# Two-layer block kernel: large-product operands placed at multiples of 512 bytes, vectors split into two tables

## The chip, the cores and the metric

The kernel runs on one core of a Trainium2 chip. The metric is the device time in microseconds (us) of one execution, as a median over runs; the profiled execution is a single one, seen through its trace. PE is TensorE, DVE is VectorE, ACT is ScalarE, POOL is GpSimd, SP is SyncE.

## The reference, cut to what matters

Two transformer-like layers for 256 tokens of width 1024, all in float32. The parts with large matrices are these:

```python
proj = h @ w_in[l]                              # layer 1: 1024 -> 2568
x = x + concat([o, pool_out]) @ w_out[l]        # 1024 -> 1024
q = (xb @ w_query)                              # 1024 -> 2048
...                                             # top 16 of 128 x 128 experts for each of 8 heads
u = expert_down[idx]; v = expert_up[idx]        # 16384 experts of width 1024
act = gelu(einsum("td,thkd->thk", xb, u))
y = einsum("thk,thkd->td", gate * act, v)
...
proj = h @ w_in_2                               # layer 2: 1024 -> 3584
x = x + mix @ w_out_2
u = causal_dwconv(h @ w_up, conv_w, conv_b)
x = x + (gelu(u) * (h @ w_gate)) @ w_down       # 1024 -> 2816 -> 1024
g = sigmoid(rmsnorm(x) @ w_ple_gate);  x = x + (p @ w_ple) * g
```

The kernel computes the expert layer densely: all 16384 experts for all tokens, multiplied by a table of gates that is zero where an expert was not chosen.

## The kernel before, in words

All large matrices lie in memory as 412 tiles of 128 x 1024 float32 (512 KB). SP loads them in one order into four slots, `raw`. For each tile ACT writes the rounded part `whi` (type fp32r, `split_hi`) and DVE the rest `wlo = raw - whi` (`split_lo`), both in rings of four slots. The activations are split in the same way: `ahi`/`alo` for an operand of 1024 features, `phi`/`plo` (two slots of 256 tokens each) for the products of the expert layer's second half and of the feed-forward layer's second half, `pthi`/`ptlo` for the small embedding product. Each product of float32 numbers is then three products of fp32r (`products`): high x high, high x low, low x high.

A tile is used in one of two ways:

- `gemm_tile`: the weights are stationary. For each of 8 slices `k`, the 128 x 128 slice of `whi` or `wlo` is loaded into the array and 256 columns of `ahi`/`alo` are streamed: 24 products of 128x256 for each tile. Layer 1's input (20 tiles), the queries (16), the experts' first half (128), layer 2's q, k and retention parts (20) and the feed-forward layer's first half (44) go this way.
- `token_rows`: the activations are stationary. A 128 x 128 slice of `ahi`/`alo` or `phi`/`plo` is loaded and 512 columns of `whi`/`wlo` are streamed: 12 products of 128x512 for each tile. With `ahi` stationary: the output projections and the values (8 tiles each) and most of the last gate. With `phi` stationary: the experts' second half (128 tiles) and the feed-forward layer's second half (22 tiles).

There is no scheduler: each engine's program is written out in order and waits on counting semaphores. The matrices' order sets the stages; the list below names those that the prediction speaks of.

- Stage of the experts' first half (span's time about 220 to 600 us): PE makes `gemm_tile` after `gemm_tile`; DVE picks the top 16 and splits tiles; from the first pick on POOL issues 256 indirect DMAs (`scatter`, L409) that add the gates of one head, one choice and one block of 128 tokens each into the table `gates_dense` in memory. Before the first one of a head it waits until the previous head's have landed.
- Stage of the experts' second half (about 604 to 961 us), 128 tiles: for each tile `n` ACT copies `ea` row `n` to `phi` (`p_hi`), which waits until PE has finished tile `n - 2`; DVE makes `plo` (`p_lo`), then splits a weight tile, then multiplies row `n + 2` of `ea` with the gates in `gd` (`apply`, L1850). SP loads `gd` four tiles at a time from `gates_dense` (`gates_of`) in between the weight loads. The tokens of the second block are gated from this table only from tile `SPLIT` = 88 on: so before the pair of loads for tile 88 SP waits for all the scatters of that block (`scat1`, the wait after `up_pair`'s first loop), and everything that SP loads later, weights too, stands behind that wait.

Where the tensors lie in a partition is set by `place`: it hands out addresses one after another from the first free byte, 16512, rounding sizes up to 32 bytes. Worked out from the code, the starts before, with their remainders:

| tensor | start before | mod 512 | mod 64 |
|---|---|---|---|
| `raw`, `whi`, `wlo` | 16512, 32896, 49280 | 128 | 0 |
| `ahi`, `alo` | 65664, 73856 | 128 | 0 |
| `phi`, `plo` | 94176, 96224 | 480 | 32 |
| `pthi`, `ptlo` | 215136, 217184 | 96 | 32 |
| `ea`, and with it `h32`, `sq` | 98272, 98272, 106464 | 480 | 32 |
| `TT`, `X` (plain float32) | 193472, 181184 | 448 | 0 |
| `gw_hi` (8 columns a slice) | 218048 | 448 | 0, 32 in turn |

All slices of `whi`, `ahi` and `phi` that the products take begin a multiple of 512 bytes behind the tensor's start, so a slice has the remainder of its tensor.

Of the kernel before, what the change touches and what calls it, by code (L numbers as in the profile page):

```python
# [16 lines left out]
F32R = mybir.dt.float32r  # L17
F16 = mybir.dt.float16
U32 = mybir.dt.uint32
ALU = mybir.AluOpType  # L20
# [4 lines left out]
T = 256  # L25
TB = T // P
D = 1024
KT = D // P
# [47 lines left out]
CV = {}  # L76
_c = 0
for _n, _w in (("norm_mix", KT), ("conv", 48), ("dn_norm", 1), ("pool_scale", PG), ("norm_ffn", KT), ("norm_mid", KT),
# [2 lines left out]
    CV[_n] = _c  # L81
    _c += _w
N_CV = _c

# [13 lines left out]
def program(nc, x_tok, vecs, wts, c1, gate_w, rows, w_pool, keys, c2, ple_t, nrows, out):  # L100
    ctx = ExitStack()
    with ctx:
        s = {n: ctx.enter_context(nc.semaphore("s_" + n)) for n in SEMS}


        top = [-(-nc.sbuf_base // 32) * 32]
        slab = ctx.enter_context(nc.sbuf_tensor("slab", [P, (nc.sbuf_bytes_remaining - 64) // 4], F32))

        def place(name, shape, dt=F32, at=None):
            size = int(np.prod(shape)) * (2 if dt == F16 else 4)  # L110
            size = -(-size // 32) * 32
            if at is None:
                at, top[0] = top[0], top[0] + size
            else:
                at[0], at = at[0] + size, at[0]
            return nc.alloc_sbuf_tensor_at(name, [P] + list(shape), dt, offset=at)

        raw = place("raw", [2, 2 * TW])
        whi = place("whi", [RING, TW], F32R)
        wlo = place("wlo", [RING, TW], F32R)  # L120
# [1 line left out]
        alo = place("alo", [KT, T], F32R)  # L122
        ident = place("ident", [P])
        ones = place("ones", [P])
        vec = place("vec", [N_CV])
        warm = place("warm", [8])
        wm = place("wm", [KT])
        eps = warm[:, 6:7]
        small = top[0]
        xt = place("xt", [TB, D])  # L130
        pf = place("pf", [2, T])
        aux_end = top[0]
        phi = place("phi", [2, T], F32R)
        plo = place("plo", [2, T], F32R)
        aux = [small]
        v16 = place("v16", [TB, 2, TOPK], at=aux)
        i16 = place("i16", [TB, 2, TOPK], U32, at=aux)
# [12 lines left out]
        aux = [small + 4 * KT * T]  # L150
# [3 lines left out]
        aux = [small]  # L154
# [2 lines left out]
        iota = place("iota", [P, GT], F16, at=aux)  # L157
        oh1 = place("oh1", [2, 2, SPLIT, GT], F16, at=aux)
        assert aux[0] <= small + 4 * KT * T
        aux = [aux_end]  # L160
        oh2 = place("oh2", [2, P, GT], F16, at=aux)
        oheq = place("oheq", [2, SPLIT, GT], F16, at=aux)
        assert aux[0] <= top[0]
        aux = [small]
        gd = place("gd", [2, 4, T], at=aux)
        assert aux[0] <= small + 4 * KT * T
        arena = top[0]
        ea = place("ea", [N_EXP, T])
        end = top[0]
        assert end <= nc.sbuf_usable_end, end  # L170

        a = [arena]
        h32 = place("h32", [KT, T], at=a)
# [55 lines left out]
        c = 0  # L229
# [55 lines left out]
            return bank((0, 1, 6, 7, 2, 3, 4, 5)[b0], n, base)  # L285

        def vcol(name, j=0):
            return vec[:, CV[name] + j:CV[name] + j + 1]

        def b3(ap, n):  # L290

# [25 lines left out]
        def _(sp):  # L317
            sp.dma_start(xt[:, 0, :], x_tok[:, 0, :]).then_inc(s["x_in"], 16)
            sp.dma_start(xt[:, 1, :], x_tok[:, 1, :]).then_inc(s["x_in1"], 16)
            sp.dma_start(vec[:, :], vecs).then_inc(s["vec_in"], 16)  # L320
            rs = (s["raw0"], s["raw1"], s["raw2"], s["raw3"])
            for j in range(4):
                if j == 1:
# [108 lines left out]
        def split_hi(act, u, j, quad=None):  # L432

            if quad is None:
                if u >= N_TILES:
                    return
                act.wait_ge((s["raw0"], s["raw1"], s["raw2"], s["raw3"])[j], 16 * (u // 4 + 1))
                if u >= RING:
                    act.wait_ge(s["w_used"], u - RING + 1)
            else:  # L440
                act.wait_ge((s["raw0"], s["raw1"], s["raw2"], s["raw3"])[j], quad * 16 + 16)
                act.wait_ge(s["w_used"], quad * 4 + (j - RING + 1))
            nc.scalar.activation(whi[:, j, :], raw_tile(j // 2, j % 2), ACT.Copy).then_inc(s["w_hi"], 1)  # L443

        def split_lo(dve, u, j, quad=None):

            if quad is None:
                if u >= N_TILES:
                    return
                dve.wait_ge(s["w_hi"], u + 1)  # L450
                if u >= RING:
                    dve.wait_ge(s["w_used"], u - RING + 1)
            else:
                dve.wait_ge(s["w_hi"], quad * 4 + (j + 1))
                dve.wait_ge(s["w_used"], quad * 4 + (j - RING + 1))
            nc.vector.tensor_tensor(wlo[:, j, :], raw_tile(j // 2, j % 2), whi[:, j, :].bitcast(F32),  # L456
                                    ALU.subtract).then_inc(s["w_lo"], 1)
# [75 lines left out]
        def turned_dve(dve, n, q, weight):  # L533
# [5 lines left out]
            m.then_inc(s["operand"], 1)  # L539

        mix_weight = lambda k: vcol("norm_mix", k)
        peer_weight = lambda k: vcol("norm_ffn", k)
        mid_weight = lambda k: wm[:, k:k + 1]
        ffn_weight = lambda k: vcol("ffn_norm", k)
        ple_weight = lambda k: vcol("ple_norm", k)

# [559 lines left out]
        def _(act):  # L1106
# [21 lines left out]
            act.wait_ge(s["t_pre"], 1)  # L1128
            row_root(0, 1, 2, pre[:, 0, 0:1])
            split_hi(act, 0, 0)  # L1130
            act.wait_ge(s["vec_in"], 16)
            for q in range(4):
                turned_act(act, 0, q, mix_weight)
            for u in range(1, LEAD):
# [357 lines left out]
        def _(dve):  # L1492
            V = nc.vector
            ch = Chain(dve, s["dve_step"])
# [24 lines left out]
                V.tensor_scalar(half_row(h32_t, b0), half_row(xt, b0), r_col[:, 0, 1:2], None, ALU.mult)\  # L1519
                 .then_inc(s["yd"], 1)  # L1520
            split_lo(dve, 0, 0)
            dve.wait_ge(s["vec_in"], 16)
            for q in range(4):
                turned_dve(dve, 0, q, mix_weight)
            for u in range(1, LEAD):
# [2 lines left out]
            def lo_for(u):  # L1528
                split_lo(dve, u + LEAD, (u + LEAD) % 4)

            ch(V.tensor_tensor(wm[:, :], vec[:, CV["norm_mid"]:CV["norm_mid"] + KT],
                               vec[:, CV["attn_norm"]:CV["attn_norm"] + KT], ALU.mult))
            bv = lambda n: col[n].rearrange("p (n h) -> p n h", n=TB)
            bav = col["ba"].rearrange("p (n c) -> p n c", n=TB)

# [653 lines left out]
```

## Time and profile before

| what | value |
|---|---|
| median of three runs | 1329.02 us (1328.91 to 1329.16) |
| span of the profiled execution, first to last instruction | 1327.4 us |
| PE busy with matmuls | 1310.4 us, 99% of the span |
| PE loading stationary operands | 1196.9 us, 90% |
| DVE / ACT / POOL busy | 943.1 / 725.3 / 517.7 us |
| memory traffic | 253.03 MB, mean 191 GB/s |
| granted TensorE clock, mean | 0.998 |

No other time of the profiled execution is recorded than its span; the median of the runs is 1.6 us above it. The busy time of PE is a sum of overlapping instructions: a matmul's shown duration is its latency, and the next one starts before it ends. How fast PE works is therefore read from the distance between the starts of matmuls, or from their count in a stretch.

### The profile page before, as it was taken

Reading aid. Unit: us, or ns where it says so; the run is one execution under the profiler, and the core shown is the slowest. Engines: PE = TensorE matmul, PEld = TensorE weight load, DVE = VectorE, ACT = ScalarE, POOL = GpSimd, SP = SyncE. Lnnn points to the kernel's source line nnn. Section 1 sums busy time; section 2 is a strip of 40 time slices with the busy share of each in tenths; the row PEclk is TensorE's granted clock in tenths of the full one; section 3 lists DMA queues with packets and bytes.
Section 4 is the critical chain, followed back from the end, with each engine's and each line's share of the span. In section 5 each row is a group of like instructions: output and inputs, shape, how many; then the busy total and the mean of one; then the engine's idle time right before and its main releaser. Section 6 shows DMA issues by size and latency. Waiting matters only on the chain. (4 is left out here: it accounts for less than half of the span.)

```text
span 1327.4 us, 26387 instructions
## 1 busy us (share of the span) xinstructions
PE 1310.4 (99%) x8853; PEld 1196.9 (90%) x8853; DVE 943.1 (71%) x1766; ACT 725.3 (55%) x1077; POOL 517.7 (39%) x276
## 2 busy tenths in 40 slices
PE   8999999999999999999999999999999999999997
PEld 8999899999999999998888888788789888999986
DVE  6885677999998467766666666666666667676665
ACT  6833557777777743344444444444465446444446
POOL 1010002888887888787787778100000000000000
PEclk9999999999999999999999999999999999999999
DMA  7459554777767766668777778777674335555551
GB/s 257 149 194 383 197 175 154 180 185 184 183 177 186 191 168 153 142 146 216 209 208 211 213 213 209 262 234 228 213 242 162 112 115 183 181 188 183 184 191 64
DMA packets 119325, 253.03 MB, mean 191 GB/s; under 512 B 44336, under 2 KB 60848, under 8 KB 118752
## 3 DMA queue, kind: packets, MB, share of 16 engines
q1 hardware_dynamic: 77232, 229.24, 53.5%
q0 software_dynamic: 42032, 22.99, 10.9%
q8 instruction: 36, 0.59, 0.2%
q14 instruction: 25, 0.20, 0.0%
HBM read 234.23 MB, written 17.96 MB: 190 GB/s over the span
## 5 line engine op out<-in xcount | busy, mean ns | idle before, releaser
L456 DVE TENSOR_TENSOR wlo<-raw,whi 128x1024 fp32r<-128x1024 f32 x412 | 503.1, 1223 | 156.3 <-ACT whi L443 147.5
L443 ACT ACTIVATE whi<-raw 128x1024 fp32r<-128x1024 f32 x412 | 435.1, 1058 | 305.8 <-PE ps L462 292.8
L409 POOL DMA_INDIRECT gates_dense<-gate,spot x256 | 506.1, 1977 | 170.2 <-issue 78.7
L460 PE MATMUL ps<-ahi,whi 128*128 128x256 f32 x1824 | 522.5, 286 | 2.9 <-DVE alo L537 2.6
L461 PE MATMUL ps<-alo,whi 128*128 128x256 f32 x1824 | 515.9, 283 | 0.0
L462 PE MATMUL ps<-ahi,wlo 128*128 128x256 f32 x1824 | 515.7, 283 | 0.0
L460 PEld LDWEIGHTS ps<-ahi,whi 128*128 128x128 f32 x1824 | 349.9, 192 | 7.5 <-issue 5.8
L461 PEld LDWEIGHTS ps<-alo,whi 128*128 128x128 f32 x1824 | 349.4, 192 | 0.9
L462 PEld LDWEIGHTS ps<-ahi,wlo 128*128 128x128 f32 x1824 | 349.4, 192 | 0.0
L460 PE MATMUL ps<-whi,phi 128*128 128x512 f32 x600 | 238.2, 397 | 1.2 <-DVE plo L1854 1.1
L462 PE MATMUL ps<-whi,plo 128*128 128x512 f32 x600 | 237.8, 396 | 0.0
L461 PE MATMUL ps<-wlo,phi 128*128 128x512 f32 x600 | 237.7, 396 | 0.0
L1854 DVE TENSOR_TENSOR plo<-ea,phi 128x256 fp32r<-128x256 f32 x128 | 54.5, 426 | 126.9 <-ACT phi L1289 120.2
L460 PEld LDWEIGHTS ps<-whi,phi 128*128 128x128 f32 x600 | 113.0, 188 | 28.8 <-issue 1.1
L462 PEld LDWEIGHTS ps<-whi,plo 128*128 128x128 f32 x600 | 113.0, 188 | 27.5
L461 PEld LDWEIGHTS ps<-wlo,phi 128*128 128x128 f32 x600 | 113.1, 188 | 26.5
L1278 ACT ACTIVATE ea<-ps 128x256 f32 x120 | 46.1, 384 | 134.5 <-PE ps L462 134.3
L460 PE MATMUL ps<-whi,ahi 128*128 128x512 f32 (+1 forms) x136 | 52.4, 385 | 0.1
L461 PE MATMUL ps<-wlo,ahi 128*128 128x512 f32 (+1 forms) x136 | 51.3, 377 | 0.0
L462 PE MATMUL ps<-whi,alo 128*128 128x512 f32 (+1 forms) x136 | 51.3, 377 | 0.0
L427 POOL DMA_DIRECT2D wrow<-in_nrows x1 | 0.6, 580 | 126.6 <-DVE plo L1854 126.6
L1289 ACT ACTIVATE phi<-ea 128x256 fp32r x120 | 47.9, 399 | 0.0
(367 smaller groups left out, 1088.0 us busy)
## 6 DMA issues: line engine op xcount, KB each, us to landing
raw<-in_wts SPq DMA_DIRECT2D x412, 512.0 KB, 3.7
gates_dense<-pf POOLq DMA_DIRECT2D x4, 4096.0 KB, 30.8
gd<-gates_dense SPq DMA_DIRECT2D x22, 256.0 KB, 4.8
gd<-gates_dense SPq DMA_DIRECT2D x10, 512.0 KB, 5.8
gates_dense<-gate,spot POOLq DMA_INDIRECT x256
cst<-in_c POOLq DMA_DIRECT2D x1, 1216.0 KB, 6.5
xt<-in_x_tok SPq DMA_DIRECT2D x2, 512.0 KB, 4.5
kk<-in_keys POOLq DMA_DIRECT2D x1, 1024.0 KB, 5.2
```

Source lines behind the costliest of these rows:

```text
L409: pl.indirect_dma_start(out=dense, out_offset=bass.IndirectOffsetOnAxis(ap=spot[:, tb, h, k:k + 1], axis=0), in_=gate[:, tb, h, k:k + 1], ...
L427: pl.dma_start(wrow[:, :, :].rearrange("p a n -> p (a n)"), nrows.partition_broadcast(P)).then_inc(s["nrows_in"], 16)
L443: nc.scalar.activation(whi[:, j, :], raw_tile(j // 2, j % 2), ACT.Copy).then_inc(s["w_hi"], 1)
L456: nc.vector.tensor_tensor(wlo[:, j, :], raw_tile(j // 2, j % 2), whi[:, j, :].bitcast(F32), ALU.subtract).then_inc(s["w_lo"], 1)
L460: nc.tensor.matmul(out_ap, wh, xh, start=first, stop=False, skip_group_check=True)
L461: nc.tensor.matmul(out_ap, wh, xl, start=False, stop=False, skip_group_check=True)
L462: return nc.tensor.matmul(out_ap, wl, xh, start=False, stop=last, skip_group_check=True)
L1278: A(row_of(quad * 4 + n), late(n if four else n % 2, T), ACT.Gelu).then_inc(s["gelu"], 1)
L1289: A(phi[:, n % 2, :], row_of(quad * 4 + n), ACT.Copy).then_inc(s["p_hi"], 1)
L1854: V.tensor_tensor(plo[:, n % 2, :], row_of(oct_ * 8 + n), phi[:, n % 2, :].bitcast(F32), ALU.subtract)\
```

## The change

The tensors are placed anew; no instruction of the five engines changes its place or its shape, except that the load of the vectors is now two loads.

- A first table `vec_a` (89 columns, 356 bytes, given 384) lies at 16512, and the address behind it is rounded up to a multiple of 512. From there `raw`, `whi`, `wlo`, `ahi`, `alo`, `ident`, `ones`, then `phi` and `plo` (which lay behind `xt` and `pf`), then `xt`, `pf` and the arena `ea` each begin at a multiple of 512.
- The second table `vec_b` (104 columns), `warm` and `wm` lie behind `ea`, at the end of the memory.
- SP loads `vec_a` and `vec_b` by a DMA each; ACT and DVE wait for both at the place where they waited for one.

Worked out from the code, the starts after: `raw` 16896, `whi` 33280, `wlo` 49664, `ahi` 66048, `alo` 74240, `phi` 83456, `plo` 85504, `ea` 97792, all with remainder 0 mod 512; `pthi` 214656 has 128 mod 512 and 0 mod 64; `TT` 192992 and `X` 180704 have 480 mod 512 and 32 mod 64.

```diff
@@ -81,6 +81,9 @@
 N_CV = _c
+N_CV_A = CV["ffn_norm"]
+N_CV_B = N_CV - N_CV_A
+assert N_CV_A <= 96
@@ -115,6 +118,8 @@
+        vec_a = place("vec_a", [N_CV_A])
+        top[0] = -(-top[0] // 512) * 512
         raw = place("raw", [2, 2 * TW])
         whi = place("whi", [RING, TW], F32R)
         wlo = place("wlo", [RING, TW], F32R)
@@ -122,16 +127,14 @@
         ident = place("ident", [P])
         ones = place("ones", [P])
-        vec = place("vec", [N_CV])
-        warm = place("warm", [8])
-        wm = place("wm", [KT])
-        eps = warm[:, 6:7]
+        parts = top[0]
+        phi = place("phi", [2, T], F32R)
+        plo = place("plo", [2, T], F32R)
+        parts_end = top[0]
         small = top[0]
         xt = place("xt", [TB, D])
         pf = place("pf", [2, T])
         aux_end = top[0]
-        phi = place("phi", [2, T], F32R)
-        plo = place("plo", [2, T], F32R)
...
         ea = place("ea", [N_EXP, T])
         end = top[0]
-        assert end <= nc.sbuf_usable_end, end
+        vec_b = place("vec_b", [N_CV_B])
+        warm = place("warm", [8])
+        wm = place("wm", [KT])
+        eps = warm[:, 6:7]
+        assert top[0] <= nc.sbuf_usable_end, top[0]
...
         def vcol(name, j=0):
-            return vec[:, CV[name] + j:CV[name] + j + 1]
+            c = CV[name] + j
+            return vec_a[:, c:c + 1] if c < N_CV_A else vec_b[:, c - N_CV_A:c - N_CV_A + 1]
...
-            sp.dma_start(vec[:, :], vecs).then_inc(s["vec_in"], 16)
+            sp.dma_start(vec_a[:, :], vecs[:, 0:N_CV_A]).then_inc(s["vec_in"], 16)
+            sp.dma_start(vec_b[:, :], vecs[:, N_CV_A:]).then_inc(s["vec_in"], 16)
...
-            act.wait_ge(s["vec_in"], 16)
+            act.wait_ge(s["vec_in"], 32)
...
-            dve.wait_ge(s["vec_in"], 16)
+            dve.wait_ge(s["vec_in"], 32)
```

The one place where an engine's list of instructions differs is the start of SP's queue, ahead of the weight loads. Before:

```order
L316 UNCONDITIONAL_BRANCH
L318 DMA xt<-in_x_tok 128x1024
L319 DMA xt<-in_x_tok 128x1024
L320 DMA vec<-in_vecs 128x193
L325 DMA raw<-in_wts 128x1024 x4
```

The same place after the change:

```order
L324 UNCONDITIONAL_BRANCH
L326 DMA xt<-in_x_tok 128x1024
L327 DMA xt<-in_x_tok 128x1024
L328 DMA vec_a<-in_vecs 128x89
L329 DMA vec_b<-in_vecs 128x104
L334 DMA raw<-in_wts 128x1024 x4
```

The load of 193 columns is replaced by one of 89 and one of 104, and the first weight load stands one issue later.

## Rows read from the trace of the kernel before

**Rows 1.** The page: busy time of the engines, and the granted clock in 40 slices.
```profile
PE 1310.4 (99%) x8853; PEld 1196.9 (90%) x8853; DVE 943.1 (71%) x1766; ACT 725.3 (55%) x1077; POOL 517.7 (39%) x276
...
PEclk9999999999999999999999999999999999999999
```

**Rows 2.** Waits of PE: longest entry; us in total, times, longest.
```profile
PE ps L460 <- DVE alo L537: 2.6, 3, 1.3
```

**Rows 3.** Stretches: bounds, length, busy us with count (x) by engine, clock, DMA, GB/s.
```profile
250.00:450.00 200.00, 200.00 (x1669) 200.00 (x1668) 171.35 (x437) 148.22 (x188) 169.25 (x89) 1.00 0.72 183
620.00:820.00 200.00, 200.00 (x855) 160.77 (x855) 125.57 (x213) 97.35 (x144) 159.21 (x73) 1.00 0.79 210
```

**Rows 4.** Line L460 on PE: duration ns min/median/max, first and last start us.
```profile
L460 PE MATMUL ps<-ahi,whi x1824: 277/283/387, 11.5 to 1285.2; 128*128 128x256 f32 x183
...
L460 PE MATMUL ps<-whi,phi x600: 392/397/500, 604.7 to 1290.8; 128*128 128x512 f32 x150
...
L460 PE MATMUL ps<-whi,ahi x136: 277/389/793, 130.1 to 1317.9; 128*128 128x512 f32 x120, 128*128 128x256 f32 x16
...
L460 PE MATMUL ps<-ahi,gw_hi x8: 276/276/280, 17.9 to 20.3; 128*8 128x256 f32 x8
...
L460 PE MATMUL ps<-whi,pthi x8: 393/396/479, 1097.0 to 1294.5; 128*128 128x512 f32 x8
```

**Rows 5.** Timeline of PE, two products with `ahi` stationary, 48 products apart.
```profile
137.05 0.39 PE L461 MATMUL ps<-wlo,ahi 128*128 128x512 f32 x1
...
147.93 0.39 PE L461 MATMUL ps<-wlo,ahi 128*128 128x512 f32 x1
```

**Rows 6.** Lines L692 and L740 on PE, plain float32 products, as rows 4.
```profile
L692 PE MATMUL ps<-TT,X x96: 275/275/334, 89.8 to 119.0; 128*128 128x128 f32 x96
...
L740 PE MATMUL ps<-ones,sq x16: 272/275/275, 128.4 to 130.1; 128*128 128x128 f32 x16
```

**Rows 7.** Waits of SP's queue: us in total, times, longest.
```profile
SPq L331 <- DVE wlo L456: 995.2, 406, 47.5
...
SPq L365 <- DMA gates_dense<-gate,spot: 3.9, 1, 3.9
```

**Rows 8.** Timeline of SP: start, us, what, in the window 822 to 848 us.
```profile
824.70 8.76 SPq L335 DMA_DIRECT2D raw<-in_wts  x4
837.82 0.38 SPq L343 DMA_DIRECT2D gd<-gates_dense  x1
```

**Rows 9.** Timelines of ACT and of all engines, 840 to 847 us; in brackets idle time before.
```profile
841.20 1.06 ACT L443 ACTIVATE whi<-raw 128x1024 fp32r<-128x1024 f32 x1 [1.45 <-PE ps L462]
...
844.76 1.06 ACT L443 ACTIVATE whi<-raw 128x1024 fp32r<-128x1024 f32 x1 [2.19 <-DMA raw<-in_wts]
...
846.15 0.42 DVE L1854 TENSOR_TENSOR plo<-ea,phi 128x256 fp32r<-128x256 f32 x1 [1.80 <-ACT phi L1289]
...
846.63 0.19 PEld L460 LDWEIGHTS ps<-whi,phi 128*128 128x128 f32 x1 [0.29 <-DVE plo L1854]
```

**Rows 10.** The scatters on POOL: all 256 (ns), then single ones.
```profile
L409 POOL DMA_INDIRECT gates_dense<-gate,spot x256: 1541/1804/2607, 221.4 to 831.8; - x128
...
613.86 1.54 POOL L409 DMA_INDIRECT gates_dense<-gate,spot  x1 [4.40 <-DMA gates_dense<-gate,spot]
...
631.24 1.54 POOL L409 DMA_INDIRECT gates_dense<-gate,spot  x1 [0.30 <-issue]
...
829.01 2.50 POOL L409 DMA_INDIRECT gates_dense<-gate,spot  x1 [0.30 <-issue]
831.82 2.51 POOL L409 DMA_INDIRECT gates_dense<-gate,spot  x1 [0.30 <-issue]
```

**Rows 11.** Timelines of the start: SP's load of the vectors, its second weight load, ACT.
```profile
1.67 0.42 SPq L320 DMA_DIRECT2D vec<-in_vecs  x1
...
8.25 0.33 SPq L325 DMA_DIRECT2D raw<-in_wts  x1
8.26 1.06 ACT L443 ACTIVATE whi<-raw 128x1024 fp32r<-128x1024 f32 x1
```

More of the change, by code:

```diff
@@ L159, in program @@
         assert aux[0] <= small + 4 * KT * T
-        aux = [aux_end]
+        aux = [parts]
         oh2 = place("oh2", [2, P, GT], F16, at=aux)
         oheq = place("oheq", [2, SPLIT, GT], F16, at=aux)
-        assert aux[0] <= top[0]
+        assert aux[0] <= parts_end
         aux = [small]
@@ L1529, in lo_for @@
                 split_lo(dve, u + LEAD, (u + LEAD) % 4)
-            ch(V.tensor_tensor(wm[:, :], vec[:, CV["norm_mid"]:CV["norm_mid"] + KT],
-                               vec[:, CV["attn_norm"]:CV["attn_norm"] + KT], ALU.mult))
+            mid, attn = CV["norm_mid"], CV["attn_norm"]
+            ch(V.tensor_tensor(wm[:, :], vec_a[:, mid:mid + KT], vec_a[:, attn:attn + KT], ALU.mult))
             bv = lambda n: col[n].rearrange("p (n h) -> p n h", n=TB)
```

## The prediction

> **What bounds the kernel now.** I read the page first: PE has matmuls in flight for 1310.4 of 1327.4 us and the clock stands at nine tenths or more in all 40 slices, which is the 2.4 GHz level [rows 1]. The list of PE's waits comes next, and its longest entry is 2.6 us in total [rows 2]. So PE waits for nobody that matters, and the time is the number of products times the distance between their starts. That distance is the number to look for, and the durations do not give it directly, since they overlap. The table of stretches does: between 250 and 450 us PE started 1669 products of 128x256 in 200 us, one each 119.8 ns; between 620 and 820 us it started 855 of 128x512 in 200 us, one each 233.9 ns [rows 3]. At 2.4 GHz, 256 columns last 106.7 ns and 512 last 213.3 ns. So each product costs about 13 ns more than its columns in the first case and 20.6 ns in the second, and the question is what of this surplus hangs on addresses.
>
> **What the rows say about addresses.** There are three kinds of stationary operand among the fp32r products.
> With `phi` stationary (480 mod 512, 32 mod 64) the distance is 233.9 ns. With `ahi` stationary (128 mod 512, 0 mod 64) and the very same moving operand `whi`, 48 products take 147.93 - 137.05 = 10.88 us, 226.7 ns each [rows 5]. The surplus is 20.6 against 13.4 ns. The median durations have the same step: 397 ns with `phi`, 389 with `ahi` [rows 4]. That could be the stage and not the address (other work runs beside it), so I look for a second tensor at an odd address: `pthi` (96 mod 512, 32 mod 64), used in two other places, has 396 ns [rows 4]. Two tensors at 32 mod 64 are slow, one at 0 mod 64 is not, in different stages. I take the cause to be that a stationary slice of 512 bytes that starts at an odd multiple of 32 costs 7.2 ns more to fetch beside the moving stream.
> A third point gives the size of the fetch itself: with `gw_hi` stationary, only 8 columns, a 128x256 product has 276 ns where `gemm_tile`'s has 283 [rows 4]. So a full slice at 0 mod 64 costs about 7 ns over a nearly empty one, and one at 32 mod 64 about 14: twice. Doubling is what I would expect where each aligned piece becomes two; it says that 128 mod 512 is already whole pieces, and that going on to 0 mod 512 gives nothing more. This last step is inference: no fp32r operand at 0 mod 512 is in the trace. From below its worth is nothing, from above it is the 7 ns of the row with 8 columns.
> Plain float32 products do not show the step at all: `TT` (0 mod 64) and `sq` (32 mod 64) stationary both have a median of 275 ns [rows 6]. So the tensors that the change moves to 32 mod 64 (`TT`, `X`, the q and k of layer 2) lose nothing; the bound is 7 ns for some 600 products, 4 us, and I take zero as the row says.
>
> The Trainium skill has a rule that speaks against the change: "SBUF — State Buffer", Door 1: The DMA port swizzle, says that the memory has 16-byte cachelines and that the price lies in crossing to a new line. By that rule 480 is as good as 0, every operand here being at a multiple of 32, and the sum would be nothing; the step between the rows for `phi` and `ahi` disagrees with that reading.
>
> **The change part by part.**
> *The experts' second half:* 128 tiles x 12 products = 1536, each 7.2 ns less: 11.1 us. Of these 86 tiles (7.4 us) come before the wait described below, 42 tiles (3.6 us) behind it.
> *The feed-forward layer's second half:* 22 x 12 = 264 products x 7.2 = 1.9 us, PE being the bound there too.
> *The embedding:* 24 products x 7 ns, 0.2 us.
> *All `gemm_tile`s and the products with `ahi`:* from 128 to 0 mod 512, nothing, as argued.
> *The first load.* The second weight load is issued at 8.25 us, when the first has landed, and ACT's first split starts at 8.26 [rows 11]: the start of all the work hangs on that landing. One more issue ahead of it costs SP 0.42 us [rows 11]; a part of the landing is bytes in flight, which don't change, so between 0 and 0.45 us; I take 0.3 us lost. The two vector loads themselves are hidden: they are asked for only after the first split.
> *The wait for the scatters, and what is late next.* This is where a gain can be lost again. SP waited 3.9 us for the last scatter to land, once, against 995 us of waiting for free `raw` slots [rows 7]. It issued four weight loads until 833.5 us and the gates' load only at 837.82 [rows 8]. Behind it stand the weight loads of the next tiles. The effect arrives at 844.76: ACT idles 2.19 us for a `raw` tile where a step before it idled 1.45 us for PE, so it is 0.74 us late; DVE's `plo` at 846.15 is late by the same, and PE's next load of a stationary slice at 846.63 had waited 0.29 us for it [rows 9]. So PE has no reserve left at this point: what it gains before it is worth only as much as the last scatter comes earlier.
> Does it? The scatters last 1541 ns at least and 2607 at most, the last one starting at 831.8 us [rows 10]. In this stage they mostly come 2.81 us apart (829.01, 831.82), which is exactly a tile's period, 12 x 233.9 ns; others take 1.54 us [rows 10]. POOL has no semaphore with DVE or PE here, so the lockstep must come from a resource that DVE's instructions of each tile hold: a scatter that meets them lasts until they are over. Over the stage, from 613.86 to 831.82 us, 80 scatters take 218 us, 2.72 us each [rows 10]. If the whole pattern follows the tile's period (2.807 to 2.721 us, 3.1%), the last scatter comes 6.7 us earlier; if only the two thirds that are spaced by a full period do, 53 x 0.086 = 4.6 us; if none does, zero. I take 5.5, between the first two, because the repeated 2.81 is what the rows show.
>
> That POOL and DVE can hold each other up is also in the Trainium skill ("SBUF — State Buffer", Who interferes with whom): a DVE instruction with two operands in this memory contends with a GpSimd instruction that reads it. By this rule the trace agrees, since `wlo` and `plo` are such instructions; it does not change the sum.
>
> *Sum:* 5.5 (of the 7.4 before the wait) + 3.6 + 1.9 + 0.2 - 0.3 = 10.9 us. From the profiled span, 1327.4 - 10.9 = 1316.5; the median of the runs lies 1.6 us above the span, so 1318.1 us.
> Bounds of this case: nothing gained before the wait gives 1323.6 and 0.15 more for the start, about 1324; all of it gained and a free start gives 1316; with a nanosecond or so less on the aligned products too (5900 of them), about 1312.
>
> **The rivals.**
> *B, the multiple of 512 is worth something by itself.* For it: even at 0 mod 64 there are 13 ns of surplus, and the row with 8 columns shows that 7 of them hang on the stationary fetch. Against: the doubling above, and that no row has such an address. Full price: all products at the surplus of the 8-column row. Before the first scatter (221.4 us) some 860 products gain 7 ns, 6 us; from there to tile 88 only what the scatters give back, 5.5 us; behind it 42 tiles x 12 x 14 ns = 7.1, 64 tiles of `gemm_tile` (1536 products) 10.8, some 290 with `ahi` 2.0, and 264 with `phi` 3.7: 35 us, 1294. At half that price about 1307.
> *C, the change does nothing to the speed.* The slowness with `phi` would then come from what runs beside it or from rewriting `phi` for each tile. For it: the durations with `ahi` spread from 277 to 793 ns [rows 4], so other things than the address play in. Against: `pthi`, written once, is as slow. Time: 1329.0 plus up to 0.3 for the start. This is also what the 16-byte rule gives.
> *D, slower.* With all operands at 0 mod 512, the stationary and the moving slice begin at the same place of whatever the memory is divided into, and all products get `phi`'s surplus. Against: before, `ahi` and `whi` both stood at 128 mod 512, also equal, and are the fast ones. For it: nobody has seen 0. Price: 5520 products of 128x256 and 360 with `ahi` x 7.2 ns = 42 us, no gain on `phi`: 1371. It decides from the point where the aligned products lose over 1.9 ns each (10.9 us over 5880).
>
> **How the numbers follow.** My forecast 0.65, B 0.13, C 0.13, D 0.09. A measurement of this kernel tells about 0.2%, 2.7 us, from no change. Faster: the forecast and B, 0.78; same: C, 0.13; slower: D, 0.09. The forecast's own range is 1312 to 1324. To hold 8 in 10 the range reaches down into B's half price, 1304, and up over C, 1330; outside are B at full price and D.
>
> **What would show it.** In the changed kernel: 120 ns between starts in 250 to 450 us, as before (B: nearer 113; D: 127); about 226.7 ns, 882 products in 200 us, where `phi` is stationary, and a median duration near 389 instead of 397; 283 for `gemm_tile`. SP's one wait for the scatters grows from 3.9 us to between 4 and 11, and a wait of PE of about 2 us appears once near 840 us. If PE's wait there is over 7 us the scatters did not move with the tiles; if the distance with `phi` is still 234 ns, the address was not the cause. The start of the first split should move by at most 0.45 us.

## The result and the profile after

The changed kernel takes 1332.89 us (median of 10 runs, 1331.43 to 1334.80) against 1329.23 before (10 runs, 1328.85 to 1329.85): ratio 1.0028, 95% interval 1.0019 to 1.0036. It is slower, by about 3.7 us, and its profiled span is 1329.8 us against 1327.4. Its line numbers from `split_hi` on are 9 higher than before (L460 is L469, L409 is L418).

The page of the changed kernel, busy time and clock in 40 slices, to be held against [rows 1]:

```profile
PE 1299.7 (98%) x8853; PEld 1197.4 (90%) x8853; DVE 942.3 (71%) x1766; ACT 725.2 (55%) x1077; POOL 526.2 (40%) x276
...
PEclk9999999999999999999999999799999999999998
```

PE was busy for 10.7 us less in a longer span, and one slice of the clock, the 26th, has dropped to 7. So the products did become faster, and one hole has opened. The same two stretches as in [rows 3], after the change:

```profile
250.00:450.00 200.00, 200.00 (x1669) 200.00 (x1668) 171.29 (x437) 148.20 (x188) 169.91 (x89) 1.00 0.73 183
620.00:820.00 200.00, 200.00 (x884) 165.58 (x884) 130.00 (x222) 100.00 (x147) 161.39 (x70) 1.00 0.80 218
```

The first half of the experts' work is the same to the product (1669). In the second half 884 instead of 855 products fit in 200 us, 226.2 ns each instead of 233.9. Line L469 of the changed kernel by operands (durations in ns, minimum, median, maximum), as [rows 4]:

```profile
L469 PE MATMUL ps<-ahi,whi x1824: 277/283/388, 11.6 to 1287.6; 128*128 128x256 f32 x183
L469 PE MATMUL ps<-whi,phi x600: 387/389/796, 604.5 to 1293.2; 128*128 128x512 f32 x150
L469 PE MATMUL ps<-whi,ahi x136: 277/389/793, 130.2 to 1320.3; 128*128 128x512 f32 x120, 128*128 128x256 f32 x16
...
L469 PE MATMUL ps<-whi,pthi x8: 392/398/479, 1100.3 to 1296.8; 128*128 128x512 f32 x8
```

The products with `phi` went from 397 to 389. But `pthi`, which the change also moved from 32 to 0 mod 64, stayed slow: 398. The prediction's rule said 389 for it.

The hole is in PE's timeline of the changed kernel (start us, duration us, in brackets the idle time before):

```profile
838.33 0.39 PE L471 MATMUL ps<-whi,plo 128*128 128x512 f32 x1
852.29 0.80 PE L469 MATMUL ps<-whi,phi 128*128 128x512 f32 x1 [13.57 <-DVE plo L1863]
852.88 0.63 PE L470 MATMUL ps<-wlo,phi 128*128 128x512 f32 x1
853.30 0.63 PE L471 MATMUL ps<-whi,plo 128*128 128x512 f32 x1
...
855.36 0.40 PE L470 MATMUL ps<-wlo,phi 128*128 128x512 f32 x1
```

Between 838.33 and 852.29 us PE started nothing, 13.7 us more than a usual distance. The first products behind the hole start about 0.43 us apart instead of 0.227. The table of stretches shows why (columns as in [rows 3]):

```profile
850.00:852.00 2.00, 0.00 (x0) 0.00 (x0) 0.19 (x1) 1.59 (x3) 0.00 (x0) 0.50 0.99 365
852.00:856.00 4.00, 3.71 (x10) 3.03 (x11) 3.51 (x6) 1.03 (x2) 0.00 (x0) 0.59 1.03 383
```

After the idle time the granted clock stands at 0.50, the 1.2 GHz level. The seven products up to 855.36 take 3.07 us instead of 1.59, another 1.5 us. Together the hole costs 15.2 us.

SP's waits of the changed kernel (us in total, times, longest), as [rows 7], tell what SP waited for:

```profile
SPq L340 <- DVE wlo L465: 976.7, 402, 47.5
...
SPq L374 <- DMA gates_dense<-gate,spot: 16.8, 1, 16.8
```

The one wait for the last scatter grew from 3.9 to 16.8 us. All 256 scatters of the changed kernel, as the first of [rows 10]:

```profile
L418 POOL DMA_INDIRECT gates_dense<-gate,spot x256: 1541/2117/2581, 221.3 to 839.8; - x128
```

The first starts where it started before (221.3 us against 221.4), the last at 839.8 us against 831.8, 8.0 us later. PE's last product ahead of the hole started at 838.33 us; this is the same product (counted from the stage's first) in the kernel before:

```profile
846.38 0.40 PE L462 MATMUL ps<-whi,plo 128*128 128x512 f32 x1
```

SP's first load of gates behind its wait, in the changed kernel (before: 837.82 us, [rows 8]):

```profile
843.19 0.38 SPq L352 DMA_DIRECT2D gd<-gates_dense  x1
```

PE came to this place at 838.33 us instead of 846.38, 8.05 us sooner; SP could go on only at 843.19 instead of 837.82, 5.37 us later. From SP's load to PE's next product it then took 9.1 us instead of 8.8 (before, that product started at 846.63). The three differences together make the hole's 13.7 us. (The last scatter starts 8.0 us later but SP goes on only 5.4 us later: before, 3.5 us passed from the scatter's end to SP's load, now 1.8.) The start of the kernel was no matter: ACT's first split starts at 8.32 us instead of 8.26.

### The profile page after: what moved, and what is told of

Its sections match the earlier page's. It is cut to its first block and busy times, and to the rows that moved or that the text cites. A ratio compares the mean times of both kernels' runs of the same rounds, so it can differ in the third digit from the quotient of the medians.

```text
span 1329.8 us, 26388 instructions
## 1 busy us (share of the span) xinstructions
PE 1299.7 (98%) x8853; PEld 1197.4 (90%) x8853; DVE 942.3 (71%) x1766; ACT 725.2 (55%) x1077; POOL 526.2 (40%) x276
## 3 DMA queue, kind: packets, MB, share of 16 engines
q0 software_dynamic: 42032, 22.99, 10.7%
## 5 line engine op out<-in xcount | busy, mean ns | idle before, releaser
L418 POOL DMA_INDIRECT gates_dense<-gate,spot x256 | 514.7, 2011 | 168.6 <-issue 78.3
L469 PE MATMUL ps<-ahi,whi 128*128 128x256 f32 x1824 | 522.6, 287 | 3.1 <-DVE alo L546 2.7
L469 PEld LDWEIGHTS ps<-ahi,whi 128*128 128x128 f32 x1824 | 349.8, 192 | 7.6 <-issue 5.1
L469 PE MATMUL ps<-whi,phi 128*128 128x512 f32 x600 | 234.8, 391 | 14.5 <-DVE plo L1863 14.3
L470 PE MATMUL ps<-wlo,phi 128*128 128x512 f32 x600 | 234.2, 390 | 0.0
L471 PE MATMUL ps<-whi,plo 128*128 128x512 f32 x600 | 234.0, 390 | 0.0
L469 PEld LDWEIGHTS ps<-whi,phi 128*128 128x128 f32 x600 | 113.1, 188 | 38.5 <-DVE plo L1863 14.2
L469 PE MATMUL ps<-whi,ahi 128*128 128x512 f32 (+1 forms) x136 | 52.4, 385 | 0.2 <-DVE alo L546 0.2
```

Of the source, the lines that this page charges most:

```text
L418: pl.indirect_dma_start(out=dense, out_offset=bass.IndirectOffsetOnAxis(ap=spot[:, tb, h, k:k + 1], axis=0), in_=gate[:, tb, h, k:k + 1], ...
L469: nc.tensor.matmul(out_ap, wh, xh, start=first, stop=False, skip_group_check=True)
L470: nc.tensor.matmul(out_ap, wh, xl, start=False, stop=False, skip_group_check=True)
L471: return nc.tensor.matmul(out_ap, wl, xh, start=False, stop=last, skip_group_check=True)
```

## Why the scatters came later

Before any further run, the two traces show the mechanism. The timeline of the kernel before, DVE and POOL, around one place where scatters run free:

```profile
626.46 1.22 DVE L456 TENSOR_TENSOR wlo<-raw,whi 128x1024 fp32r<-128x1024 f32 x1
626.58 2.51 POOL L409 DMA_INDIRECT gates_dense<-gate,spot  x1 [0.30 <-issue]
...
629.39 1.26 DVE L456 TENSOR_TENSOR wlo<-raw,whi 128x1024 fp32r<-128x1024 f32 x1
629.39 1.54 POOL L409 DMA_INDIRECT gates_dense<-gate,spot  x1 [0.30 <-issue]
...
631.24 1.54 POOL L409 DMA_INDIRECT gates_dense<-gate,spot  x1 [0.30 <-issue]
```

A scatter that starts 0.12 us into DVE's weight split takes 2.51 us; one that starts together with it or between two splits takes 1.54. The held one ends at 629.09, 2.63 us after the split's start, and the next scatter starts 0.30 us later: 2.93 us after the split's start. The next split comes 2.81 us after the last, so the scatter is 0.12 us into it again. That is the lockstep of one scatter a tile. Once in the loop of eight tiles DVE is 0.12 us late (629.39 instead of 629.27): then the scatter starts together with the split and is not held, and three scatters fit in two tiles. In both traces a held scatter ends 1.41 to 1.42 us after the split that it met: 629.09 is 1.41 us behind 627.68.

The same view of the changed kernel, with a usual tile and then the late one of the loop:

```profile
666.42 1.22 DVE L465 TENSOR_TENSOR wlo<-raw,whi 128x1024 fp32r<-128x1024 f32 x1
666.64 2.41 POOL L418 DMA_INDIRECT gates_dense<-gate,spot  x1 [0.30 <-issue]
...
669.14 1.22 DVE L465 TENSOR_TENSOR wlo<-raw,whi 128x1024 fp32r<-128x1024 f32 x1
669.36 2.42 POOL L418 DMA_INDIRECT gates_dense<-gate,spot  x1 [0.30 <-issue]
...
671.98 1.22 DVE L465 TENSOR_TENSOR wlo<-raw,whi 128x1024 fp32r<-128x1024 f32 x1
672.08 2.54 POOL L418 DMA_INDIRECT gates_dense<-gate,spot  x1 [0.30 <-issue]
```

The period is 2.72 us, so the scatter stands 0.22 us inside each split (666.64 against 666.42). The loop's 0.12 us are no longer enough: at 672.08 it is still 0.10 inside, and is held. Before, nine scatters started in eight tiles; now eight do. Of the 82 scatters that start after 604 us, 24 took less than 1.7 us before and 8 do now. So shorter tiles set fewer scatters free. This is the theory of the lockstep; it predicts that delaying one split in eight by 0.25 us more sets scatters free, and that delaying every split does not.

## The experiments

Every kernel was timed beside the kernel before on the same chip.

**One thing alone: `phi` and `plo` at 0 mod 64, 128 mod 512.** From the kernel before; weights, `ahi` and the arena stay where they were. What lies between (vectors, `xt`, and the gates' tables over it) moves by 4096 bytes and so keeps its remainder mod 512; the one-hot tables `oh2` and `oheq` lie over `phi` and move with it.

```diff
+        parts = top[0]
+        phi = place("phi", [2, T], F32R)
+        plo = place("plo", [2, T], F32R)
+        parts_end = top[0]
         vec = place("vec", [N_CV])
...
-        phi = place("phi", [2, T], F32R)
-        plo = place("plo", [2, T], F32R)
...
-        aux = [aux_end]
+        aux = [parts]
...
```

> The kernel before with one thing moved: phi and plo now lie in front of the vectors, at 128 mod 512 and 0 mod 64; all other operands of the large products, the gates' tables and the arena keep their old addresses. If the remainder mod 64 of the stationary slice is the whole matter and the late scatters follow from the faster tiles, this kernel behaves like the changed one: 226.7 ns between products with phi, the last scatter near 840 us instead of 832, a wait of PE of about 13 us, 1332 to 1334 us. If the multiple of 512 matters, the products with phi are slower than 226.7 ns. If the scatters are late because the gates' tables were moved, they end near 832 or earlier here, PE waits 7 us at most, and the time is about 1318 to 1322 us.

Measured: 1332.97 us, ratio 1.0027 (1.0016 to 1.0038), the changed kernel's time. Its stretch and its scatters:

```profile
620.00:820.00 200.00, 200.00 (x884) 165.60 (x883) 129.82 (x221) 99.95 (x147) 161.83 (x70) 1.00 0.79 217
```
```profile
L411 POOL DMA_INDIRECT gates_dense<-gate,spot x256: 1542/2135/2582, 221.7 to 840.3; - x128
```

884 products, last scatter at 840.3, and PE waited 14.2 us once. The place of `phi` alone makes both effects. Neither the multiple of 512 nor a new remainder of the gates' tables (480 here, as before) is needed for the late scatters.

**The rest alone: weights and `ahi` at multiples of 512, `phi` at 32 mod 512.** From the changed kernel.

```diff
+        warm = place("warm", [8])
         parts = top[0]
         phi = place("phi", [2, T], F32R)
...
-        warm = place("warm", [8])
```

> The changed kernel with the eight columns of warm placed in front of phi, so that raw, whi, wlo, ahi and alo stay at multiples of 512 and phi, plo, the gates' tables and the arena begin at 32 mod 64. If 512 is worth nothing for the operands already at 0 mod 64: 120 ns for the products of 128x256, 234 ns with phi stationary, scatters ending near 832 us, and 1329 to 1330 us, the time before with at most 0.4 us for the second load of vectors. If 512 is worth something: under 119 ns in the experts' first half and a time under 1325.

Measured: 1328.08 us, ratio 0.9990 (0.9981 to 0.9999): about a tenth of a per cent faster, a little under the 1329 to 1330 expected. 1669 products in 250 to 450 us as ever, last scatter at 831.4 us; in 620 to 820 us 859 products, 232.8 ns each, against 855 before. A multiple of 512 brings nothing to the products of weights and `ahi`.

**The scatters' end taken away.** The changed kernel without the last head's scatters for the second block of tokens; it leaves these gates out of the sum.

```diff
-            for q in range(ahead, NH * TOPK):
+            for q in range(ahead, (NH - 1) * TOPK):
...
-            sp.wait_ge(s["scat1"], 16 * TOPK * NH)
+            sp.wait_ge(s["scat1"], 16 * TOPK * (NH - 1))
```

> The changed kernel without the last 16 of the 128 scatters of the second token block, and with the wait for them lowered to 112; the gates of one head are missing for these tokens. If the scatters' end is what eats the gain, SP's wait for them and PE's wait of 13.7 us are gone, the clock stays at full, and the time is 13 us under the time before, 1315.5 to 1317. If PE would lose the time anyway (a weight load or the gates' loads too slow at the new pace), a wait of several us remains and the time stays over 1322.

Measured: 1316.81 us, ratio 0.9906 (0.9890 to 0.9922), as expected. No wait of SP for scatters and no hole: the wait is the whole loss, and without it the changed kernel is 12.5 us faster than the kernel before.

**One split in eight moved.** In the changed kernel:

```diff
                 u = W_UP + n + LEAD
+                if n == 0:
+                    idle = row_of(oct_ * 8 + (n - 1 if 0 < n < 6 else (5, 0, 0, 0, 0, 0, 12, 14)[n]))
+                    V.tensor_scalar(idle, idle, 1.0, None, ALU.mult)
                 if not last or n < 7:
                     split_lo(dve, None, u % 4, oct_ * 2 + u // 4)
```

> The changed kernel with one more small DVE instruction (a row of 256 columns times 1.0, about 0.25 us) between plo and the weight split in one of eight tiles of the experts' second half, in DVE's idle time. Theory of the lockstep: a scatter that starts while DVE splits a weight tile is held until that instruction is over and ends 1.42 us later, so that the next one starts 2.94 us after the split's start, which is 0.22 us into the next split; the loop's boundary delays one split in eight by only 0.12 us. With 0.25 more at the same place the delay exceeds 0.22, a scatter gets free once in each eight tiles, several take 1.54 us, and the last one starts at or before 832 us; the time falls to 1316 to 1322. If the rate of the scatters hangs on the share of time in which DVE is busy, more DVE work makes them no faster: last scatter at 840 or later, 1332 or more.

Measured: 1317.89 us, ratio 0.9914 (0.9898 to 0.9929). DVE and POOL at the late tile of the loop in this kernel:

```profile
672.46 0.29 DVE L1875 TENSOR_SCALAR ea<-ea  x1
672.56 1.60 POOL L418 DMA_INDIRECT gates_dense<-gate,spot  x1 [0.30 <-issue]
672.66 1.22 DVE L465 TENSOR_TENSOR wlo<-raw,whi 128x1024 fp32r<-128x1024 f32 x1
...
674.47 1.54 POOL L418 DMA_INDIRECT gates_dense<-gate,spot  x1 [0.31 <-issue]
```

The split starts at 672.66, 0.10 us behind the scatter, and does not hold it. The scatter takes 0.06 us more than 1.54 and ends at 674.16, 1.41 us after the end of the added instruction (672.75): so it seems to have been held by that one, for 0.06 us. The next scatter takes 1.54. Of the 82 scatters after 604 us 25 took less than 1.7 us, against 8. The last scatter of this run starts at 824.9 us. Adding work to DVE in 16 places made the kernel 15 us faster than the changed one.

**Every split moved.** The same instruction in each tile, on rows that nobody reads at the time.

> The changed kernel with the small DVE instruction ahead of the weight split in every tile of the experts' second half instead of one in eight. By the lockstep all splits are then late by the same amount, the distance between them stays 2.72 us except for the 0.12 us at the loop's boundary, and no scatter gets free: one scatter a tile, the last one near 840 us, a wait of PE of some 13 us, 1331 to 1335 us. If the gain of the one in eight came from anything that an added instruction does as such, eight times as many do at least as well: 1318 or less.

Measured: 1334.26 us, ratio 1.0050 (1.0030 to 1.0069); last scatter at 840.5 us, a hole of 14.0 us; 9 of the 82 scatters took less than 1.7 us. It is one split's distance to the next that counts, not the added work. The rival that DVE's share of busy time sets the scatters' rate falls too: with one in eight DVE did more and the scatters ended sooner.

**The same instruction in the kernel before.**

> The kernel before with the small DVE instruction in one of eight tiles, at the same place. Before, scatters already get free once in eight tiles and PE is the bound with the 233.9 ns of phi at 32 mod 64, so the instruction brings nothing by itself: last scatter at 832 us or a little earlier, 1328 to 1330 us. If the instruction helps otherwise than by the scatters' end, it shows here: under 1326.

Measured: 1329.53 us, ratio 1.0002 (0.9992 to 1.0012), last scatter at 829.5. By itself it is worth nothing.

**The split in two halves.** In the changed kernel, in the experts' second half only:

```diff
-            nc.vector.tensor_tensor(wlo[:, j, :], raw_tile(j // 2, j % 2), whi[:, j, :].bitcast(F32),
-                                    ALU.subtract).then_inc(s["w_lo"], 1)
+            w = TW // parts_of
+            for q in range(parts_of):
+                c = slice(q * w, (q + 1) * w)
+                m = nc.vector.tensor_tensor(wlo[:, j, c], raw_tile(j // 2, j % 2)[:, c], whi[:, j, c].bitcast(F32),
+                                            ALU.subtract)
+            m.then_inc(s["w_lo"], 1)
...
-                    split_lo(dve, None, u % 4, oct_ * 2 + u // 4)
+                    split_lo(dve, None, u % 4, oct_ * 2 + u // 4, 2)
```

> The changed kernel with DVE's split of a weight tile made by two instructions of 512 columns each in the experts' second half. If a scatter is held only until the instruction that it meets is over, it gets free after at most 0.65 us, takes 1.9 to 2.2 us instead of 2.4, and the last one starts well before 832 us: no wait of PE, 1315.5 to 1318 us. If back-to-back DVE instructions hold it as one would, the scatters stay at one a tile and the time at 1331 to 1335.

Measured: 1316.71 us, ratio 0.9907 (0.9890 to 0.9923). The last scatter starts at 790.6 us, 49 us sooner, and neither SP nor PE waits for it. One that meets the first half of a split:

```profile
634.01 0.68 DVE L468 TENSOR_TENSOR wlo<-raw,whi 128x512 fp32r<-128x512 f32 x1
634.30 1.81 POOL L418 DMA_INDIRECT gates_dense<-gate,spot  x1 [0.30 <-issue]
634.62 0.68 DVE L468 TENSOR_TENSOR wlo<-raw,whi 128x512 fp32r<-128x512 f32 x1
```

It ends at 636.11, 1.42 us after the end of the first half (634.69), though the second half goes on until 635.30. So a scatter is held only by the instruction that it meets.

**`ahi` at 32 mod 64.** This was meant to confirm the prediction's rule, and refuted it. In the changed kernel, `warm` in front of `ahi` and `wm` behind `alo`; that also puts `phi` and `plo` at 64 mod 512, which the expectation took to be harmless.

```diff
+        warm = place("warm", [8])
         ahi = place("ahi", [KT, T], F32R)
         alo = place("alo", [KT, T], F32R)
+        wm = place("wm", [KT])
```

> The changed kernel with warm (32 bytes) in front of ahi and wm behind alo, so that ahi and alo begin at 32 mod 64 and all else at 0 mod 64. ahi is moving in the products of 128x256 and stationary in 360 of 128x512. If only the stationary slice counts: 120 ns in the experts' first half as before, about 234 ns where ahi is stationary, 2 to 3 us more than the changed kernel, 1334 to 1337. If the moving operand counts too: the first half slows by up to 7 ns a product, 127 ns, and the time rises by up to 40 us.

Measured: 1313.88 us, ratio 0.9888 (0.9871 to 0.9904), 20 us under the expectation, and 14.2 us less than with the weights at 0, `phi` at 32 and `ahi` at 0 (1328.08). Its stretches, then line L469 by operands:

```profile
250.00:450.00 200.00, 200.00 (x1716) 200.00 (x1716) 173.09 (x434) 151.06 (x192) 171.54 (x89) 1.00 0.74 190
...
620.00:820.00 200.00, 200.00 (x858) 161.12 (x857) 126.01 (x215) 97.75 (x144) 158.72 (x75) 1.00 0.80 210
```
```profile
L469 PE MATMUL ps<-ahi,whi x1824: 277/280/390, 11.6 to 1269.3; 128*128 128x256 f32 x183
L469 PE MATMUL ps<-whi,phi x600: 392/393/497, 594.0 to 1274.8; 128*128 128x512 f32 x150
```

The 128x256 products became faster, 116.6 ns instead of 119.8 (1716 against 1669). The products with `phi`, now at 64 mod 512, a multiple of 64, are slow again: 858 in 200 us, 233 ns. The second contradicts "32 mod 64 is slow"; the first is a gain that the rule has no place for, since it says nothing of the moving operand. (With `ahi` stationary at 32 the median is 395 ns, which either rule would give.) What fits all rows is the difference between the remainders mod 512 of the two operands: `phi` at 480 with `whi` at 128 slow, at 128 with 128 fast, at 0 with 0 fast, at 32 with 0 and at 64 with 0 slow; `pthi` at 96 with 128 and at 128 with 0 slow. For 128x512 products equal is better; for 128x256 ones it is worse.

**All operands equal, at 32 mod 512.** The test of this new theory. In the changed kernel, `warm` stands in front of `raw`.

> The changed kernel with warm (32 bytes) in front of raw, so that raw, whi, wlo, ahi, alo, phi, plo and the arena all begin at 32 mod 512: equal to each other, none at a multiple of 64. The run with ahi alone at 32 mod 64 contradicts the prediction's rule. New theory: what counts is whether the stationary and the moving operand have the same remainder. Then this kernel is the changed one: 120 ns in the first half, 226.7 ns with phi, a wait of PE of about 13 us, 1331 to 1334 us. By the prediction's rule (32 mod 64 costs 7 ns): 234 ns with phi, 127 ns for 128x256, over 1365.

Measured: 1333.76 us, ratio 1.0036 (1.0022 to 1.0050), with a hole of 13.9 us. Line L469 of this kernel:

```profile
L469 PE MATMUL ps<-ahi,whi x1824: 277/283/388, 11.6 to 1289.3; 128*128 128x256 f32 x183
L469 PE MATMUL ps<-whi,phi x600: 389/389/792, 604.6 to 1294.9; 128*128 128x512 f32 x150
```

At 32 mod 64 throughout, and as fast as at 0: the start's own remainder counts for nothing, equality does. `phi` lies at the very address that it had in the second experiment (83488), where `whi` was at 0 and `phi` was slow.

**`phi` equal to `whi`, `ahi` apart, split in halves.** Three distances for `ahi`, by putting `warm`, or `warm` and `wm`, or these and `vec_b` in front of it; `phi` and `plo` lie right behind `wlo`.

```diff
-        ahi = place("ahi", [KT, T], F32R)
-        alo = place("alo", [KT, T], F32R)
-        ident = place("ident", [P])
-        ones = place("ones", [P])
         parts = top[0]
         phi = place("phi", [2, T], F32R)
         plo = place("plo", [2, T], F32R)
         parts_end = top[0]
+        ident = place("ident", [P])
+        ones = place("ones", [P])
+        warm = place("warm", [8])
+        ahi = place("ahi", [KT, T], F32R)
+        alo = place("alo", [KT, T], F32R)
...
```

> The changed kernel with the split in halves (run before: 1316.7), phi and plo placed behind wlo at 0 mod 512 as whi, and ahi, alo 32 bytes off. New theory: phi equal to whi gives 226.7 ns, ahi apart from whi gives 116.6 ns instead of 120.0 for the 128x256 products and 233 for the 360 with ahi stationary. Gain over 1316.7: 5472 x 3.2 ns = 17.5 us, less 2.3 us and what DVE and POOL can't follow: 1299 to 1305. If the gain of the run with ahi at 32 came from elsewhere (the scatters' end, the arena's address), 1314 to 1320.

> As f1_ahi_32_apart with ahi, alo 64 bytes off whi's remainder instead of 32. If any difference is as good, the same time within 2 us. If only a difference that is no multiple of 64 helps, 120.0 ns and about 1316.

> As f1_ahi_32_apart with ahi, alo 480 bytes off (32 below the next equal place), with vec_b, warm and wm in front. If any difference helps, the same time within 2 us; if its size or sign matters, another distance than 116.6 ns between the 128x256 products.

Measured: 32 apart 1303.73 us, ratio 0.9804 (0.9788 to 0.9820); 64 apart 1298.21, ratio 0.9768 (0.9752 to 0.9785); 480 apart 1311.06, ratio 0.9860 (0.9843 to 0.9876). Line L473 (L469 above) of the first of them:

```profile
L473 PE MATMUL ps<-ahi,whi x1824: 277/281/390, 11.7 to 1260.9; 128*128 128x256 f32 x183
L473 PE MATMUL ps<-whi,phi x600: 389/389/495, 596.6 to 1266.5; 128*128 128x512 f32 x150
L473 PE MATMUL ps<-whi,ahi x136: 277/395/796, 129.8 to 1293.8; 128*128 128x512 f32 x120, 128*128 128x256 f32 x16
```

`phi` fast, the 128x256 products a little faster, and `ahi` stationary slower (395 against 389), as the theory says. In 620 to 820 us all three have the fast `phi` (884, 880 and 884 products; the 880 have a wait of 0.8 us behind a weight load among them), and no scatter is waited for. "Any difference is as good" is refuted: the three times differ by 13 us. The distance between 128x256 products differs less in the traces: 1700, 1700 and 1693 products in 250 to 450 us, though `ahi` 32 apart had given 1716 in the kernel with `phi` at 64. The five runs of the 64-apart kernel go from 1297.6 to 1308.2 us, and the profiled one is the slowest, so its trace doesn't show why the others are faster. The version with 64 apart is the fastest measured, 31 us under the kernel before.

## Why the prediction was wrong, point by point

- **What bounds the kernel:** right. PE's distance between starts sets the time as long as nothing holds it up; taking the scatters' wait away gave 12.5 us, against 13.2 summed for the products less 0.3 for the start.
- **The size on `phi`:** right, 884 products in 200 us against 882 forecast, median 389. **Its reason:** wrong, so the size came out right by luck: the change happened to give `phi` and `whi` the same remainder. "A stationary slice that starts at an odd multiple of 32 costs 7.2 ns more" fell with `phi` at 64, which was slow, and with all at 32, which was fast. The cause is that `phi` and `whi` had different remainders. I had two tensors for the rule, `phi` and `pthi`, but both differed from `whi` as well; the rows could not tell the two rules apart, and I didn't notice. Two more readings suffer from it. The embedding's 0.2 us didn't come, since `pthi` still differs from `whi` (398 ns). And `gw_hi` differs from `ahi` too, nearly throughout, so that its 276 ns do not show what a full slice costs over an empty one. (In the plain float32 row of `TT` and `X` it is `X` that is stationary; both start at 448 mod 512, so nothing hangs on it.)
- **512 by itself (rival B):** nothing, as forecast, 1669 products in both kernels.
- **The first load:** 0.06 us on ACT's start, forecast 0.3.
- **What is late next:** this is the step that failed. The place, the wait and the lack of reserve were right: "what it gains before it is worth only as much as the last scatter comes earlier". But the scatters were taken to come 5.5 us earlier, with zero as the worst, so that 5.5 of the 7.4 us before the wait would be kept. They came later: the last one started 8.0 us later and SP went on 5.4 us later. The product ahead of the wait came 8.05 us sooner and the hole took 15.2 us, so this term was a loss of about 7 us and not a gain of 5.5. The prediction had named the sign of it, a wait of PE over 7 us, but as the case in which the scatters stay where they were. I had seen that the full period repeats (2.81 us) and not asked why some scatters in between take 1.54: that exception made the rate higher than one a tile, and it hung on 0.12 us. Here the scatters' rate, locked to DVE's tiles, did not follow the tiles' period.
- **The hole's price:** forecast at about 2 us, 7.4 at most; it was 13.7 us of idle time and 1.5 us at the halved clock. The products' 13.2 us gained (the forecast's sum) less 15.2 lost is +2.0 us, of the +2.4 us between the profiled spans.
- **The rival on the other side (D)** had the right sign by a mechanism that doesn't exist: its products did not become slower (1669 in 200 us and a median of 389 ns with `ahi`, as before). The 128x256 products are slower with equal remainders than with different ones, but they had equal ones before the change too.

Open: how far "equal" has to hold. With `phi` 32, 64 and 352 apart, `ahi` 32, 64 and 480 apart, and `pthi` 96 and 128 apart count as different; 256 was not tried, and the slices step by 512 bytes, so no run tests a larger modulus by itself. Also open is why the 128x256 products gain between 1.7 and 3.3 ns by different distances and in different kernels, why 64 apart is the fastest of them, and what part of DVE's split holds a scatter.

## What to carry to other kernels

When a change makes a bound engine faster, look for the next thing that arrives on its own schedule, and take its reserve as it is; here it was zero. If that thing runs in lockstep with another loop, find in the trace the exceptions to the lockstep and what lets them happen, before scaling its rate; a long instruction that blocks another engine can be cut in two, which here was worth 16 us (1316.71 against 1332.89) and cost nothing that shows in the time. And before a rule on an address is believed, put the addresses of all operands of the instruction in the table, not only that of the one suspected.

## What the runs showed of the hardware that was not expected

- For fp32r products with 128 stationary columns, the distance between starts depends on whether the two operands have the same remainder mod 512: 226 to 227 ns for 512 moving columns when equal, 233 to 234 when not; 120 ns for 256 moving columns when equal, and 116.6 to 118 when not. The remainder itself (0, 32 or 128 mod 512) makes no difference. Plain float32 products of 128 columns show none of this in their duration: 275 ns with `TT` and `X` both at 448, and 275 ns with `ones` at 128 and `sq` at 480 [rows 6].
- An indirect DMA's issue on GpSimd takes 1.54 us, and up to 2.5 us when it starts 0.1 us or more into DVE's subtraction of 1024 columns with both inputs in the same memory. It then ends 1.41 us after that instruction. One that starts together with the subtraction (629.39 us) or 0.1 us ahead of it (672.56 us) is not held by it. Two DVE instructions of 512 columns back to back let it through between them (last scatter at 790.6 instead of 839.8 us). The Trainium skill, "SBUF — State Buffer", Who interferes with whom, says that a DVE instruction with two inputs in this memory contends with a GpSimd instruction that reads it. The traces agree in kind, 2.41 to 2.54 us against 1.54; the lockstep that follows is shown by these runs alone.
- After 13.6 us without a product the granted clock was 0.50, the 1.2 GHz level, and the next seven products took 3.07 us instead of 1.59.
